# 22 fp32 products of constants per layer, placed at five points between the gating unit and the recurrence

## The chip, the cores and the metric

The kernel runs on one core of one Trainium2 chip. The metric is the device time of one launch in microseconds (us), as the median of several runs. TensorE multiplies matrices into PSUM (8 banks of 128 x 512 fp32), VectorE and ScalarE do the elementwise work and copy out of PSUM, SyncE and GpSimd issue DMAs. The engines run their own instruction streams in order and wait for one another on semaphores.

## The reference

A two-layer block (attention, mLSTM, windowed attention) is followed by a second two-layer block, the last block here. Only the middle of each of its layers matters. From the projection `h = x @ w_in` three units are formed side by side:

```
out_a = spatial_gating(gelu(a_u), gelu(a_v), ...)      # layer_norm over 256 features, then w (4 heads, 128x128) @ v
out_b = gated_deltanet(...)                            # (I + L)^-1 by a triangular solve, then a recurrence over chunks
out_c = gla(...)                                       # gated linear attention: chunk states, masked scores, outputs
mix   = concatenate([out_a, out_b, out_c]) @ w_out
```

Everything is fp32 with 512 tokens and a width of 1024. The kernel solves the delta rule with chunks of 128 tokens, 8 heads: 32 triangular matrices of 128 x 128 for each layer.

## The kernel before

The program is a list of stages. Each stage has one function for TensorE, one for ScalarE, one for VectorE; after most of them stands a barrier (`end_stage`: drain, count, wait for all three). The GEMMs of the projections and of the MLPs (`gemm_pe`, L513 and L515) split fp32 into two parts and are the bulk of the time. The order of work in the stages around the change is written out by hand.

In the last block each layer `l` runs: projection, `form_pe` (L2340, the decayed key products and the matrices L), then one stage with `units_pe` and `solve_pe` on TensorE, `compact`, `units_act` and `solve_act` on ScalarE and `solve_dve` on VectorE, and then `rec_pe` (the recurrence, L2565 to L2601, with L2569 its first products).

`units_pe` (L2144) does in this order:

- L2147: two products with a matrix of ones give the sums over features of the gating unit; VectorE centres with them (L2221, L2223), ScalarE squares (L2202).
- L2151: two products of ones give the sums of squares; ScalarE makes the reciprocal root (L2205, L2206), VectorE normalises (`norm_v_dve`, L2236, L2237).
- L2156, L2161: transposes of the normed values and of the decayed keys, copied by ScalarE (L2213 to L2216).
- L2167: the seven state updates of the gated attention, read by VectorE (`gla_states_dve`, L2265, L2270).
- L2171, L2176: the gating unit's bias rows (2 rows deep) and its mixing products.
- L2183: the scores of the gated attention, 32 rows deep, masked by VectorE (`gla_mask_dve`, L2282), after a wait for the states.
- L2190, L2194: its outputs.

`solve_pe` (L2380) waits for the inverses of the 32 x 32 diagonal blocks (`so_x`), which VectorE computes row by row (`rows_dve_of_inverse`, L2509 and L2511) in between all the above and transposes at L2532. It then puts the inverse of 128 x 128 together: 32 x 32 products (L2385, L2386, L2395 to L2397), then 64 x 64 products (L2412 forms one off-diagonal part, L2403 in `corner` the next), with copies by ScalarE and VectorE (L2454, L2461, L2467, L2542, L2547) in between.

`keep_busy_pe` (L530) is already there: after the row sums that close a GEMM it runs six fp32 products of the constant matrix of ones with 512 columns of constants (L533) into a PSUM bank that nobody reads.

Of the kernel before, what the change touches and what calls it, by code (L numbers as in the profile page):

```python
# [231 lines left out]
def program(nc, xT_d, vec_d, shared_d, first_d, second_d, gup_d, sguw_d, sgub_d, crow_d, ada_d, w_d, out_d):  # L232
    with ExitStack() as ctx:
# [3 lines left out]
        def signal(name):  # L237
            return Signal(ctx.enter_context(nc.semaphore(name)))
# [26 lines left out]
        def C(name, i=0, n=P):  # L265
            if name in SHARED_AT:
                return con[:, SHARED_AT[name] + i:SHARED_AT[name] + i + n]
            at = FIRST_AT[name] if name in FIRST_AT else SECOND_AT[name]
            return con2[:, at + i:at + i + n]

        def area(at, *dims, of=arena):

            n = int(np.prod(dims))
            assert at + n <= ARENA, (at, n)
            a = of[:, at:at + n]
            if len(dims) == 2:
                return a.rearrange("p (a b) -> p a b", a=dims[0])
            if len(dims) == 3:
                return a.rearrange("p (a b c) -> p a b c", a=dims[0], b=dims[1])
            return a  # L280
# [246 lines left out]
                if "unread" in tiles[-1]:  # L527
                    keep_busy_pe(pe, tiles[-1]["unread"])

        def keep_busy_pe(pe, bank):  # L530

            for _ in range(6):
                pe.matmul(PS[:, bank, :], C("ones"), con[:, 0:512], start=True, stop=True)  # L533

        def together(tiles, n):
# [1587 lines left out]
        def vt(n, cols):  # L2123

            return Y[:, 6 + n // 2, 256 * (n % 2) + cols.start:256 * (n % 2) + cols.stop]

        bc = ada_extra[:]
        _, e1, e2, kdec = (area(4096 + 512 * i, 512) for i in range(4))
# [11 lines left out]
        def update_bank(c):  # L2140

            return PS[:, UPDATE_BANKS[c % 2][c // 4], 256 * (c // 2 % 2):256 * (c // 2 % 2) + 256]

        def units_pe(pe, l):  # L2144

            for t in range(2):
                ins = pe.matmul(PS[:, 0, :], C("ones"), vp_[:, t, :], start=(t == 0), stop=(t == 1))  # L2147
            ins.then_inc(sg_z.sem, 1)
            pe.wait_ge(sg_sq.sem, sg_sq.next("pe"))
            for t in range(2):  # L2150
                ins = pe.matmul(PS[:, 1, :], C("ones"), sq2[:, t, :], start=(t == 0), stop=(t == 1))  # L2151
            ins.then_inc(sg_t.sem, 1)
            pe.wait_ge(sg_v.sem, sg_v.next("pe"))
            for n in range(NLT):
                for t in range(2):
                    ins = pe.transpose(PS[:, 2 + n // 2, 256 * (n % 2) + P * t:256 * (n % 2) + P * t + P],  # L2156
                                       vp_[:, t, P * n:P * n + P], C("ident"))
            ins.then_inc(sg_t.sem, 1)
            pe.wait_ge(ga_prod.sem, ga_prod.next("pe"))
            for n in range(NLT):  # L2160
                ins = pe.transpose(PS[:, 5, P * n:P * n + P], kdec[:, P * n:P * n + P], C("ident"))  # L2161
            ins.then_inc(ga_kt.sem, 1)
            pe.wait_ge(sg_tc.sem, sg_tc.next("pe"))
            pe.wait_ge(ga_ktc.sem, ga_ktc.next("pe"))
            for c in range(7):
                o, n = 64 * (c % 2), c // 2
                ins = pe.matmul(update_bank(c), kdt[o:o + 64, n, :], vg[o:o + 64, n, :], start=True, stop=True)  # L2167
            ins.then_inc(ga_st.sem, 1)
            pe.wait_ge(sg_w.sem, sg_w.next("pe"))
            for q in range(2):  # L2170
                pe.matmul(PS[:, q, :].rearrange("p (n t) -> p n t", n=NLT), PAIR[0:2], bs_row[0:2, P * q:P * q + P].unsqueeze(1).to_broadcast([2, NLT, P]),  # L2171
                          start=True, stop=False, skip_group_check=True)
                for n in range(NLT):
                    for j in range(2):
                        h = 2 * q + j
                        ins = pe.matmul(PS[64 * j:64 * j + 64, q, P * n:P * n + P], vt(n, slice(64 * h, 64 * h + 64)), wsT[:, h, :],  # L2176
                                        start=False, stop=True, skip_group_check=True)
            ins.then_inc(sg_z.sem, 1)
            pe.wait_ge(ga_state.sem, ga_state.next("pe"))
            for h in range(4):  # L2180
                for n in range(NLT):
                    a, b = 32 * h, P * n
                    ins = pe.matmul(PS[:, GS[h], b:b + P], kg[a:a + 32, b:b + P], qg[a:a + 32, b:b + P], start=True, stop=True)  # L2183
                ins.then_inc(ga_s.sem, 1)
            pe.wait_ge(ga_pt.sem, ga_pt.next("pe", 4))
            for n in range(NLT):
                for p in range(2):
                    for j in range(2):
                        h = 2 * p + j
                        ins = pe.matmul(PS[64 * j:64 * j + 64, 6 + p, P * n:P * n + P], vg[:, n, 64 * h:64 * h + 64],  # L2190
                                        pTg[:, n, P * h:P * h + P], start=True, stop=False, skip_group_check=True)
                    for c in (2 * n, 2 * n + 1):
                        if c >= 1:
                            ins = pe.matmul(PS[:, 6 + p, 64 * c:64 * c + 64], Sg[:, c, P * p:P * p + P], qg[:, 64 * c:64 * c + 64],  # L2194
                                            start=False, stop=True, skip_group_check=True)
            ins.then_inc(ga_o.sem, 1)
# [116 lines left out]
        def lt(h, n, rows, cols):  # L2313

            return XH[rows, 2 * h + n // 2, P * (n % 2) + cols.start:P * (n % 2) + cols.stop]
# [8 lines left out]
        def quad(q):  # L2324
            return slice(32 * q, 32 * q + 32)
# [52 lines left out]
            so_L.advance("pe", 8)  # L2378

        def solve_pe(pe):  # L2380
            pe.wait_ge(so_x.sem, so_x.next("pe"))
            for g in range(2):
                for m in range(16):
                    h, n, i = 4 * g + m // 4, m % 4, 16 * g + m
                    pe.matmul(PS[quad(1), g, 32 * m:32 * m + 32], lt(h, n, quad(0), quad(1)), X64[quad(0), i, 0:32], start=True, stop=True)  # L2385
                    ins = pe.matmul(PS[quad(3), 2 + g, 32 * m:32 * m + 32], lt(h, n, quad(2), quad(3)), X64[quad(2), i, 0:32],  # L2386
                                    start=True, stop=True)
                ins.then_inc(so_y.sem, 1)
            pe.wait_ge(so_T.sem, so_T.next("pe"))
            pe.wait_ge(ga_out.sem, ga_out.next("pe"))  # L2390
            for g in range(2):
                pe.wait_ge(so_yc.sem, so_yc.next("pe", 2))
                for m in range(16):
                    i = 16 * g + m
                    pe.matmul(PS[quad(1), 4 + g, 32 * m:32 * m + 32], T32[quad(1), i, :], Y32[quad(1), i, :], start=True, stop=True)  # L2395
                    pe.matmul(PS[quad(2), 6 + g, 32 * m:32 * m + 32], Y32[quad(3), i, :], T32[quad(3), i, :], start=True, stop=True)
                    ins = pe.matmul(PS[quad(0), 4 + g, 32 * m:32 * m + 32], Y32[quad(1), i, :], T32[quad(1), i, :], start=True, stop=True)  # L2397
                ins.then_inc(so_off.sem, 1)

            def corner(r):  # L2400
                pe.wait_ge(so_zc.sem, so_zc.next("pe"))
                for m in range(8):
                    ins = pe.matmul(PS[LOW, 4 + r, 64 * m:64 * m + 64], Y64[TOP, 8 * (r % 2) + m, :], lt(2 * r + m // 4, m % 4, TOP, TOP),  # L2403
                                    start=True, stop=True)
                ins.then_inc(so_top.sem, 1)

            for r in range(4):
                if r % 2 == 0:
                    pe.wait_ge(so_offa.sem, so_offa.next("pe"))
                    pe.wait_ge(so_offv.sem, so_offv.next("pe", 2))  # L2410
                for m in range(8):
                    ins = pe.matmul(PS[TOP, r, 64 * m:64 * m + 64], lt(2 * r + m // 4, m % 4, LOW, TOP), X64[LOW, 8 * r + m, :],  # L2412
                                    start=True, stop=True)
                ins.then_inc(so_z.sem, 1)
                if r >= 1:
                    corner(r - 1)
            corner(3)

        so_d, so_ld, so_T = (signal(n) for n in ("solve_blocks_compact", "solve_blocks_in", "solve_inverses32_turned"))
        D_ = area(4096, 4, 512)[:, :, 0:256]  # L2420
# [488 lines left out]
```

## Time and profile before

| | |
|---|---|
| median of 3 timed runs | 3948.94 us (3947.5 to 3950.69) |
| the profiled execution | 3947.25 us, span 3945.5 us |
| TensorE busy | 3780.2 us, 96% |
| VectorE / ScalarE busy | 2107.3 / 1392.4 us |
| mean granted TensorE clock | 0.961 |
| L513, three largest groups | 2080.0 + 1755.8 + 1206.1 us |
| L533 (products of constants) | 72 records, 31.9 us |

One execution is profiled; times count from its start. Busy time of an engine is time with an instruction under way; idle time of an engine that isn't waited for costs nothing. A matmul record of fp32 covers half of a product: one `matmul` call shows as two records. The granted clock is given as a share of 2.4 GHz; it has two levels here, 1.00 (2.4 GHz) and 0.50 (1.2 GHz), and a mean over a stretch may lie between.

### The profile page before, as it was taken

How to read it: one execution, taken by the hardware profiler on the slowest of the kernel's cores; microseconds unless marked ns; L12 is line 12 of the kernel's file. 1: busy time of each engine (PE TensorE's matmuls, PEld its weight loads, DVE VectorE, ACT ScalarE, POOL GpSimd, SP SyncE). 2: the span in 40 equal slices, each digit the busy share in tenths (PEclk: the TensorE clock that was granted, in tenths of full speed). 3: DMA queues.
4: the chain of work that ended last, by engine and by line, in shares of the span. 5: the costliest groups of instructions: out<-in, count | busy, mean ns of one | idle time of the engine just before them, and what ended most of it. 6: DMA issues, size and time to landing. Idle time of an engine off the chain costs nothing.

```text
span 3945.5 us, 45029 instructions
## 1 busy us (share of the span) xinstructions
PE 3780.2 (96%) x18676; PEld 3145.5 (80%) x18676; DVE 2107.3 (53%) x3730; ACT 1392.4 (35%) x2109; POOL 86.1 (2%) x164
## 2 busy tenths in 40 slices
PE   8997989999999999999999979999999999899998
PEld 5985669999987688888887867888788877677886
DVE  5936767644457543333337477533633374765335
ACT  4424552212356432322226533222322256233222
POOL 0100001111000000000000000000000000000000
PEclk9998999999999999999999959999999999689999
DMA  6410004333220122232222201222222222002222
GB/s 221 153 50 1 22 27 134 123 127 129 102 69 23 43 96 96 96 110 98 99 96 83 80 6 43 96 97 96 88 96 96 98 84 80 22 33 89 98 97 80
DMA packets 92887, 333.37 MB, mean 84 GB/s; under 512 B 11364, under 2 KB 11532, under 8 KB 92428
## 3 DMA queue, kind: packets, MB, share of 16 engines
q1 hardware_dynamic: 77040, 278.10, 20.5%
q0 software_dynamic: 12800, 41.95, 3.4%
q10 hardware_dynamic: 2844, 10.44, 0.7%
q8 instruction: 148, 2.42, 0.2%
q14 instruction: 55, 0.45, 0.0%
HBM read 328.35 MB, written 2.10 MB: 84 GB/s over the span
## 4 chain that ended last, share of the span: by engine, by line
PE 88%; DVE 5%; ACT 5%; issue 1%; DMA 0%; DVEq 0%; ACTq 0%; SPq 0%
PE PS L513 73%; PE PS L1111 2%; PE PS L515 2%; PE PS L1129 1%; PE PS L1656 1%; PE PS L1468 1%; PE PS L1096 1%; PE PS L1099 0%; PE PS L956 0%; PE PS L1097 0%; PE PS L2565 0%; PE PS L2357 0%; PE PS L1439 0%; PE PS L726 0%; PE PS L2194 0%
## 5 line engine op out<-in xcount | busy, mean ns | idle before, releaser
L513 PE MATMUL PS<-arena_r,ring_hi 128*128 128x512 f32 (+1 forms) x6160 | 2080.0, 376 | 45.8 <-DVE H_r L690 38.9
L513 PE MATMUL PS<-arena_r,ring_r 128*128 128x512 f32 (+1 forms) x4688 | 1755.8, 375 | 0.0
L513 PEld LDWEIGHTS PS<-arena_r,ring_hi 128*128 128x128 f32 x6160 | 1153.4, 188 | 227.9 <-DVE H_r L690 30.0
L513 PE MATMUL PS<-H_r,ring_hi 128*128 128x512 f32 (+1 forms) x3216 | 1206.1, 375 | 0.0
L513 PEld LDWEIGHTS PS<-arena_r,ring_r 128*128 128x128 f32 x4688 | 883.4, 188 | 130.7
L382 DVE TENSOR_TENSOR ring_r<-ring,ring_hi 128x1024 fp32r<-128x1024 f32 x514 | 627.1, 1222 | 652.5 <-ACT ring_hi L373 652.0
L373 ACT ACTIVATE ring_hi<-ring 128x1024 fp32r<-128x1024 f32 x514 | 541.4, 1055 | 866.9 <-DMA ring<-weights_dram 859.0
L513 PEld LDWEIGHTS PS<-H_r,ring_hi 128*128 128x128 f32 x3216 | 608.3, 189 | 94.8 <-issue 3.1
L1825 ACT ACTIVATE arena<-PS 128x512 f32<-128x512 f32 x88 | 52.6, 598 | 527.5 <-PE PS L513 527.5
L1275 DVE SCALAR_TENSOR_TENSOR XH<-PS,mods,XH 128x256 f32<-128x256 f32 (+1 forms) x168 | 79.4, 518 | 235.9 <-PE PS L513 221.3
L344 DVE CAST arena_r<-arena 128x512 fp32r<-128x512 f32 (+1 forms) x184 | 74.2, 404 | 199.0 <-ACT arena L1322 195.9
L1829 DVE SCALAR_TENSOR_TENSOR arena<-arena,PS 128x512 f32<-128x512 f32 x88 | 60.5, 687 | 219.6 <-PE PS L513 219.6
L1321 ACT ACTIVATE arena<-PS 128x384 f32<-128x384 f32 (+1 forms) x96 | 49.9, 520 | 282.0 <-PE PS L513 282.0
L1836 DVE SCALAR_TENSOR_TENSOR XH<-XH,PS 128x512 f32<-128x512 f32 x64 | 44.0, 687 | 153.9 <-PE PS L513 153.9
L1293 DVE TENSOR_TENSOR arena_r<-arena,arena_r 128x512 fp32r<-128x512 f32 (+1 forms) x184 | 118.9, 646 | 6.3
L1111 PE MATMUL PS<-arena 128*128 128x512 f32 (+1 forms) x184 | 92.4, 607 | 4.7 <-ACT arena L1197 4.7
L690 DVE TENSOR_TENSOR H_r<-XH,arena_r 128x512 fp32r<-128x512 f32 (+1 forms) x144 | 91.1, 633 | 4.9
L1129 PEld LDWEIGHTS PS<-con,arena 128*128 128x128 f32 x368 | 43.1, 143 | 49.6 <-issue 39.1
L1146 DVE TENSOR_REDUCE small<-PS 128x1 f32<-128x768 f32 (+3 forms) x80 | 61.6, 770 | 30.3 <-PE PS L1099 28.8
L1184 ACT ACTIVATE arena<-PS,small 128x768 f32<-128x768 f32 (+3 forms) x80 | 59.4, 743 | 38.2 <-DVE small L1151 38.0
L1859 DVE SCALAR_TENSOR_TENSOR arena<-arena,vec 128x511 f32<-128x511 f32 (+2 forms) x72 | 53.5, 748 | 36.0 <-ACT arena L1874 34.3
L344 DVE CAST arena_r<-XH 128x512 fp32r<-128x512 f32 (+1 forms) x144 | 56.4, 391 | 20.1 <-ACTq L326 17.7
(389 smaller groups left out, 3347.1 us busy)
## 6 DMA issues: line engine op xcount, KB each, us to landing
ring<-weights_dram SPq DMA_DIRECT2D x526, 512.0 KB, 3.2
rstd<-ada_later_dram POOLq DMA_DIRECT2D x54, 256.0 KB, 2.9
mean<-ada_later_dram POOLq DMA_DIRECT2D x53, 256.0 KB, 3.0
ada_extra<-ada_later_dram POOLq DMA_DIRECT2D x53, 256.0 KB, 3.0
XH<-xT_dram ACTq DMA_DIRECT2D x1, 3072.0 KB, 20.4
ring<-weights_dram ACTq DMA_DIRECT2D x4, 512.0 KB, 4.1
out_dram<-XH SPq DMA_DIRECT2D x8, 256.0 KB, 2.0
con<-second_dram ACTq DMA_DIRECT2D x1, 1536.0 KB
```

Source lines behind the costliest of these rows:

```text
L344: return nc.vector.tensor_copy(out, src)
L373: nc.scalar.activation(ring_hi[:, n % RING, :, :], ring[:, n % RING, :, :], ACT.Copy).then_inc(hi_ready.sem, 1)
L382: nc.vector.tensor_tensor(ring_lo[:, slot, :, :], ring[:, slot, :, :], ring_hi[:, slot, :, :].bitcast(F32), ALU.subtract).then_inc(lo_read ...
L513: ins = pe.matmul(PS[:, o.bank, 0:hi - lo], w[:, 0, :], x, **flags)
L515: ins = pe.matmul(PS[:, o.bank, 0:t["n"] * P], x, w.rearrange("p a b -> p (a b)"), **flags)
L690: nc.vector.tensor_tensor(H_r[:, k, lo:hi], x, x_hi.bitcast(F32), ALU.subtract).then_inc(xlo_ready.sem, 1)
L1111: ins = pe.matmul(out_of(gi), g["v"](kts[t]), turned[gi % 2][:, t, :], start=(t == 0), stop=(t == len(kts) - 1))
L1129: ins = pe.transpose(turned_ps, p_tile, C("ident"))
L1146: v_link(dve, nc.vector.tensor_reduce(col(i, 0), s_all(i, g), AX, ALU.max))
L1275: ins = nc.vector.scalar_tensor_tensor(out=X[:, m, a:b], in0=ps[:, a - lo:b - lo], scalar=mods[:, l, s, gate + m:gate + m + 1], in1=X[:, m ...
L1293: nc.vector.tensor_tensor(h_lo(lo, hi), h(lo, hi), h_hi(lo, hi).bitcast(F32), ALU.subtract).then_inc(hidden_ready.sem, 1)
L1829: return nc.vector.scalar_tensor_tensor(out=h[:, m, :], in0=h[:, m, :], scalar=0.5, in1=ps, op0=ALU.mult, op1=ALU.mult)
```

## The change

`keep_busy_pe` gets a count `n`, six by default, and is called at five more places in each of the two layers: 3, 6 and 7 products into bank 4 in `units_pe`, 4 into bank 5 at the head of `solve_pe`, 2 into bank 0 at its end, 22 in all. Each call stands just ahead of a wait, the last one ahead of the barrier. Nothing reads what they write, and no wait and no signal is added.

```diff
-        def keep_busy_pe(pe, bank):
+        def keep_busy_pe(pe, bank, n=6):
-            for _ in range(6):
+            for _ in range(n):
                 pe.matmul(PS[:, bank, :], C("ones"), con[:, 0:512], start=True, stop=True)
...
                 ins = pe.matmul(PS[:, 0, :], C("ones"), vp_[:, t, :], start=(t == 0), stop=(t == 1))
             ins.then_inc(sg_z.sem, 1)
+            keep_busy_pe(pe, 4, 3)
             pe.wait_ge(sg_sq.sem, sg_sq.next("pe"))
             for t in range(2):
                 ins = pe.matmul(PS[:, 1, :], C("ones"), sq2[:, t, :], start=(t == 0), stop=(t == 1))
             ins.then_inc(sg_t.sem, 1)
+            keep_busy_pe(pe, 4, 6)
             pe.wait_ge(sg_v.sem, sg_v.next("pe"))
...
             ins.then_inc(sg_z.sem, 1)
+            keep_busy_pe(pe, 4, 7)
             pe.wait_ge(ga_state.sem, ga_state.next("pe"))
...
         def solve_pe(pe):
+            keep_busy_pe(pe, 5, 4)
             pe.wait_ge(so_x.sem, so_x.next("pe"))
...
             corner(3)
+            keep_busy_pe(pe, 0, 2)
```

## Rows read from the trace of the kernel before

**Rows 1.** The page: granted clock in 40 equal slices, and the chain by engine.
```profile
PEclk9998999999999999999999959999999999689999
PE 88%; DVE 5%; ACT 5%; issue 1%; DMA 0%; DVEq 0%; ACTq 0%; SPq 0%
```

**Rows 2.** Windows, layer 0: stretch, its length, busy us (records) by engine, clock, DMA.
```profile
2294.00:2299.00 5.00, 3.78 (x4) 1.17 (x4) 3.63 (x5) 1.66 (x4) 0.00 (x0) 0.50 0.01 3
2299.00:2302.00 3.00, 0.00 (x0) 0.00 (x0) 2.83 (x8) 1.06 (x2) 0.00 (x0) 0.97 0.00 0
2302.00:2306.00 4.00, 3.37 (x4) 0.97 (x4) 3.39 (x11) 1.82 (x3) 0.00 (x0) 0.57 0.00 0
2306.00:2309.40 3.40, 0.00 (x0) 0.00 (x0) 1.05 (x2) 3.37 (x7) 0.00 (x0) 1.00 0.00 0
...
2332.80:2345.40 12.60, 12.54 (x61) 8.96 (x61) 11.71 (x29) 1.06 (x1) 0.00 (x0) 0.50 0.01 1
2345.40:2353.00 7.60, 7.19 (x321) 6.98 (x320) 5.74 (x9) 5.04 (x8) 0.00 (x0) 0.50 0.02 5
2353.00:2365.20 12.20, 12.08 (x128) 11.89 (x128) 3.06 (x6) 2.87 (x6) 0.00 (x0) 0.50 0.00 1
...
2381.00:2384.50 3.50, 3.50 (x32) 3.34 (x31) 1.43 (x4) 0.77 (x2) 0.00 (x0) 0.99 0.00 0
```

**Rows 3.** Windows, layer 1, the same columns.
```profile
3401.70:3405.00 3.30, 0.23 (x1) 0.23 (x2) 3.13 (x8) 1.42 (x3) 0.00 (x0) 1.00 0.00 0
3405.00:3408.40 3.40, 3.27 (x4) 0.74 (x3) 3.02 (x11) 1.11 (x2) 0.00 (x0) 0.51 0.00 0
...
3435.00:3448.20 13.20, 12.58 (x62) 9.00 (x64) 12.31 (x29) 1.06 (x1) 0.00 (x0) 0.50 0.01 1
```

**Rows 4.** Timeline, TensorE: start, length, instruction, shapes, records; at full clock.
```profile
1370.95 5.31 PE L533 MATMUL PS<-con 128*128 128x512 f32 x12
```

**Rows 5.** Timeline, TensorE, layer 0; in brackets idle time before it.
```profile
2294.99 3.78 PE L2147 MATMUL PS<-arena,con 128*128 128x512 f32 x4 [1.43 <-DVEq L326]
2302.14 3.37 PE L2151 MATMUL PS<-XH,con 128*128 128x512 f32 x4 [3.37 <-ACT XH L2202]
2310.82 1.97 PE L2156 MATMUL PS<-con,arena 128*128 128x128 f32 x8 [5.31 <-DVE arena L2237]
...
2314.54 3.75 PE L2167 MATMUL PS<-arena 64*128 64x256 f32 x14 [0.90 <-ACT arena L2216]
2318.22 2.07 PE L2171 MATMUL PS<-scratch,con_r 2*128 2x512 f32 x2
...
2326.03 5.13 PE L2183 MATMUL PS<-arena 32*128 32x128 f32 x32
2332.86 0.70 PE L2190 MATMUL PS<-arena 128*64 128x128 f32 x4 [1.70 <-DVE arena L2282]
```

**Rows 6.** Timeline, VectorE, layer 0.
```profile
2318.40 2.22 DVE L2265 TENSOR_TENSOR arena<-PS,con 128x512 f32<-128x512 f32 x4 [1.74 <-PE PS L2167]
...
2330.33 2.48 DVE L2282 TENSOR_TENSOR arena<-PS,con 128x512 f32<-128x512 f32 x4
...
2342.10 1.95 DVE L2532 STREAM_TRANSPOSE arena<-silu_ctx 128x1024 f32<-128x1024 f32 x1
```

**Rows 7.** Chain in order of time, end of the solve and recurrence: start, length, what.
```profile
2362.10 3.06 PE PS L2403 x29
...
2365.97 1.86 PE PS L2569 x8
2367.84 3.60 PE PS L2565 x16
...
2377.57 1.97 PE PS L2601 x16
...
2382.28 1.73 PE PS L2565 x16
...
2385.20 1.02 PE PS L2601 x16
```

## The prediction

> **What bounds the kernel now.** I read the page first: TensorE is busy nearly all the span, 88% of the chain of waits is TensorE, and the granted clock is 1.00 (2.4 GHz) nearly everywhere except in two dips of the slices, one for each layer of the last block [rows 1]. So a TensorE product added anywhere is paid for, unless it lands in a wait of TensorE, and the only thing that products with unread results can give back is the granted clock of their neighbours. The change puts all 22 products of a layer inside those dips. Then I read layer 0 in stretches (layer 1 repeats it 1102.6 us later, with the same dips): while the gating unit's two ones products ran, and after them, the clock went from 0.50 to 0.97 with TensorE standing still, fell again during the next two products, and stayed at 0.50 (1.2 GHz) all the way to the recurrence [rows 2, 3]. Third, the timeline of TensorE with what ended each wait [rows 5], and last the VectorE instructions that release it [rows 6], because VectorE's inversion of 32x32 blocks (small instructions back to back) runs beside all of this and is what TensorE waits for.
>
> Times below are those of layer 0 in the profiled execution. It took 3947.25 us around a span of 3945.5; the median of the three timed runs is 3948.94, so it stands 1.7 us below.
>
> **Price of one product.** It is fp32, so it shows as two records. At 2.4 GHz 12 records took 5.31 us, the last one alone 0.59: (5.31 - 0.59) / 11 = 0.43 us a record, 0.86 us a product [rows 4]. At 1.2 GHz the same shape (L2147, L2151) took 3.78 and 3.37 us for two products with the tail [rows 5]; I take 1.71, twice the fast price. 22 products are 18.9 us a layer at full clock and 37.6 at half, against waits of TensorE of 3.37, 5.31, 0.90 and 1.70 us in this stretch [rows 5]. So they do not fit the waits as they stand: the change lives on the clock it buys. It adds no semaphore wait and nothing reads banks 4, 5 and 0 in between; but TensorE works in order, so whatever stands behind a product waits for it, and with it ScalarE and VectorE.
>
> **Part 1, 3 products before the wait for the squares.** L2147 ends at 2298.77, L2151 starts at 2302.14: 3.37 us of cover [rows 5]. The clock is up from about 2299.2 (0.97 over 2299 to 2302) [rows 2]; 3 x 0.86 = 2.6, and some 0.3 more for the first one at half clock: over at 2301.7, hidden. All at half clock they would take 5.1 and push 1.8 into the chain. With TensorE busy instead of still I expect the clock to hold through L2151, whose 3.37 us shrink to 1.9. ScalarE's root and VectorE's normalisation follow directly: -1.5 us.
>
> **Part 2, 6 products before the wait for the normed values.** L2151 now ends at 2304.0, the wait ends 1.5 earlier than before, at 2309.3; 6 x 0.86 = 5.2 ends at 2309.2. Hidden with nothing to spare; at half clock it would be late by 5. Behind it the transposes (L2156, L2161) and the state updates (L2167, 3.75 us) run at full clock, about 1.0 and 1.7 us shorter. What then is late is VectorE: before L2265 it sat idle for 1.74 us [rows 6]. That wait goes too, so L2265 starts 1.5 + 1.7 = 3.2 us earlier, at 2315.2. More can't be had there, since VectorE is then without a break up to its transposes of the inverse.
>
> **Part 3, 7 products before the wait for the states.** In the trace of before there is no wait at this place: L2183 starts where L2176 ends [rows 5]. There will be one only if the stretch L2171 to L2176 (7.8 us, 2318.22 to 2326.03) shrinks with the clock. At full clock I take 4.2: over at 2318.3, products 6.0 more, 2324.3, then L2183 in 2.8 instead of 5.13: 2327.1. VectorE reaches the first L2282, at 2330.33 before, at 2327.1 [rows 6]. Just hidden; gain still 3.2 us, no more, because VectorE sets it.
>
> **Part 4, 4 products before the wait for the inverse.** This is the step that decides. From 2327.1 to 2329.7 TensorE again stands still, after 32-row products. Before, in both layers, the clock fell in or just after the 3 us in which TensorE stood still at full clock [rows 2, 3], so I let it fall here, at about 2330. L2190 and L2194 then start at 2329.7 and run their 12.5 us at half clock, as in both layers before: TensorE busy for 12.54 of 12.60 us, clock 0.50 throughout, and no rise [rows 2, 3]. They end at 2342.2 and not at 2345.4. VectorE has the inverse ready (L2532 ended at 2344.05) at 2340.9 [rows 6]: TensorE is late already, there is no wait, and the 4 products stand wholly in the chain. 3.4 us at full clock, 6.8 at half; full-size products did raise the clock each time after 3 to 4 us [rows 2], so I take 5.5 us: L2385 starts at 2347.7, +2.3 us against before.
>
> The Trainium skill, page "TensorE: Matmul & The Clock Gate", part 1, section "What's actually happening", says that "the default state is throttled, and activity releases the throttle". Read as busy time that is against the row of L2190: busy without a break, and never released. Read so, the four products and all after them would run at full clock, and the sum would be rival B or A below.
>
> **Part 5, the solve.** Its first half is 32x32 products, 321 records in 7.19 us busy, 22 ns apart [rows 2]; between them stand ScalarE's copies. Bounds: nothing to 1.9 us if the clock is still full (half of a start part of 3.8 us); I take 0.5, since no row shows these records at full clock. The second half, 64x64 products, 12.08 of 12.20 us busy at 0.50 before [rows 2], keeps its length: such products never raised the clock, and after 32x32 products I expect it to fall. Bounds: 0 to 5 us of gain; I take 0.
>
> By the same page, section "Wait — 56ns, not 53.3ns?", the start-to-start of matmuls never drops under about 25 ns however small they are; by that the first half would gain exactly nothing. The trace has them at 22, so the rule does not hold here to the nanosecond, and by it the sum would be 0.5 us a layer larger.
>
> **Part 6, 2 products at the end.** Cover is what VectorE's last L2547 and the barrier take: from the end of L2403 at 2365.16 to L2569 at 2365.97, 0.8 us [rows 7]. The barrier waits for TensorE to drain, so all three engines wait. At half clock 3.4 + 0.1 - 0.8 = +2.7, at full clock +1.0. Return: if the clock rises after them, L2565 takes 1.73 and not 3.60 us, as it does later in the recurrence [rows 7], and L2569 loses up to 0.9. It comes part of the time and only for part of the stretch, because L2569 is eight tiny products: I take -1.5. Net +1.2.
>
> **Sum.** A layer: +2.3 - 0.5 + 1.2 = +3.0 us; two layers +6.0; 3947.25 + 6.0 = 3953.3. The moments at which the clock changes need not lie alike in other executions; that is worth a microsecond or three either way, more than the 1.7 us between the profiled run and the median, so I leave it at 3953.
>
> **Rivals.**
>
> A, full clock from L2147 to the recurrence: L2190/L2194 in 6.4 us, over at 2336.1, 4 products until 2339.5, L2385 with the inverse at 2340.9 (-4.5); the 64x64 products 5 us shorter; end products +1.0; L2569 and L2565 -2.8; L2601 1.02 for 1.97 [rows 7] and L2582 behind it by nearly as much, -1.7. That is -13 a layer, 3921. For it: the counts of products fill exactly the waits that this timeline has. Against: 12 us each of L2190 and of L2403 busy at 0.50. The page's rule named above is this rival.
>
> B, the clock holds through L2190 and is lost in the solve: -4.5 + 1.2 = -3.3 a layer, 3941. For it: the recurrence held 0.99 with products of the same kind, L2565 and L2601 [rows 2, 7]. Against: the 2.6 us of standing still just ahead.
>
> D, on the slower side: the clock is lost in part 2's tail, during the 1.3 us in which TensorE waits for ScalarE's copies ahead of L2167. Then L2265 starts at 2315.9, L2171 to L2176 need their 7.8 us until 2323.5, and the 7 products start at half clock: 3 us until the rise and 4.5 after, 2331.0, then L2183 2.8: 2333.8, the masks end at 2334.4 (2332.81 before). L2190 starts 1.6 late; some 2 us of it at full clock give 2 back, then the 4 products: L2385 at 2350.3, +4.9, and with parts 5 and 6 +5.6 a layer, 3958. It decides from the point where L2183 ends after VectorE has reached L2282. For it: before, the clock fell in just such a stretch, a wait with work beginning after it (0.57 over 2302 to 2306) [rows 2]. The extreme, no rise at all in any place, is 37.6 us a layer less what waits cover, over 20 a layer; against that stands the rise at 2299.
>
> **How the numbers follow.** Forecast 0.45 (3947 to 3957), A 0.07, B 0.18, D 0.25, something worse 0.05. A measurement of this kernel tells about 0.2%, 7.9 us, from no change, that is below 3941.0 or above 3956.8. Faster: A and half of B and a little, 0.20. Slower: most of D, the worse case and the forecast's upper edge, 0.32. Same: 0.48. The range that leaves out A, the worst and the edge of D is 3938 to 3965.
>
> **What would show it.** Right: clock near 1.00 from 2299 to about 2329, L2151 near 1.9 us, L2265 about 3 us earlier, 0.50 over L2190, and no idle time after the 4 products ahead of L2385, which starts 2 us late; L2569 2 to 5 us late. Wrong, towards faster: L2190/L2194 under 10 us, or a wait of TensorE before L2385. Wrong, towards slower: 0.50 over L2171 and an L2183 that VectorE waits for.

## The result, and the profile after

The change takes 3953.62 us, median of 20 runs, against 3947.55 us before, 20 runs on the same chips: ratio 1.0018, 95% interval [1.0012, 1.0024], 6.1 us slower. The forecast was 3953. Single runs of either kernel fall in two groups some 8 us apart (before: 3938 to 3942 and about 3948; after: 3945 to 3946 and 3952 to 3957), and two of the profiles below, e3's and e7's, show the difference ahead of layer 0, in code that all these kernels share, so where a few microseconds matter I read the profiles by layer as well. The profiled execution took 3953.63 us, its span is 3951.8.

L2147 keeps its number, those behind it are shifted: L2151 is L2152, L2156 is L2158, L2167 is L2169, L2171 is L2173, L2176 is L2178, L2183 is L2186, L2190 and L2194 are L2193 and L2197, L2385 is L2389, L2403 is L2407, L2412 is L2416, L2569 is L2574, L2565 is L2570, L2601 is L2606; on VectorE L2265 is L2268, L2282 is L2285, L2532 is L2537.

The timeline of TensorE in layer 0 after, which answers to [rows 5]:

```profile
2298.44 3.03 PE L533 MATMUL PS<-con 128*128 128x512 f32 x6
2302.01 1.98 PE L2152 MATMUL PS<-XH,con 128*128 128x512 f32 x4 [0.55 <-ACT XH L2205]
2303.84 5.31 PE L533 MATMUL PS<-con 128*128 128x512 f32 x12
2309.31 1.09 PE L2158 MATMUL PS<-con,arena 128*128 128x128 f32 x8 [0.16 <-DVE arena L2240]
...
2312.16 1.96 PE L2169 MATMUL PS<-arena 64*128 64x256 f32 x14 [1.32 <-ACT arena L2219]
...
2318.20 6.28 PE L533 MATMUL PS<-con 128*128 128x512 f32 x14
2324.41 2.82 PE L2186 MATMUL PS<-arena 32*128 32x128 f32 x32
2329.64 0.65 PE L2193 MATMUL PS<-arena 128*64 128x128 f32 x4 [2.42 <-DVE arena L2285]
...
2341.99 6.04 PE L533 MATMUL PS<-con 128*128 128x512 f32 x8
2347.96 0.21 PE L2389 MATMUL PS<-arena,XH 32*32 32x32 f32 x1
...
2367.70 3.45 PE L533 MATMUL PS<-con 128*128 128x512 f32 x4
2371.23 1.05 PE L2574 MATMUL PS<-arena,con_r 8*128 8x4 f32 x8
```

Three things are to be seen. The first three groups of products (3.03, 5.31, 6.28 us) have gone into waits: behind the first two TensorE still waits 0.55 and 0.16 us, behind the third not at all, because L2186 follows at once. Where no product was put it waits 1.32 us (ahead of L2169) and 2.42 us (ahead of L2193). The fourth group (6.04 us) has no wait behind it: L2389 follows at once. And the last stands between the solve and the recurrence, 3.45 us where the barrier had left 0.8 us [rows 7].

VectorE, which answers to [rows 6], has no idle time before L2268 any more, and everything on it is 3.2 us earlier:

```profile
2315.17 2.22 DVE L2268 TENSOR_TENSOR arena<-PS,con 128x512 f32<-128x512 f32 x4
...
2327.11 2.48 DVE L2285 TENSOR_TENSOR arena<-PS,con 128x512 f32<-128x512 f32 x4
...
2338.89 1.95 DVE L2537 STREAM_TRANSPOSE arena<-silu_ctx 128x1024 f32<-128x1024 f32 x1
```

The windows after, which answer to [rows 2], with the same columns (the clock is the third number from the right):

```profile
2302.00:2326.00 24.00, 22.51 (x112) 12.28 (x113) 21.42 (x51) 7.11 (x11) 0.00 (x0) 1.00 0.00 1
2326.00:2329.70 3.70, 1.28 (x18) 1.09 (x17) 3.70 (x7) 0.00 (x0) 0.00 (x0) 1.00 0.00 0
2329.70:2342.00 12.30, 12.30 (x61) 8.84 (x61) 11.41 (x28) 1.06 (x1) 0.00 (x0) 0.50 0.00 0
2342.00:2348.00 6.00, 6.00 (x11) 2.35 (x13) 4.19 (x6) 0.00 (x0) 0.00 (x0) 0.60 0.00 0
2348.00:2353.20 5.20, 4.50 (x318) 4.24 (x317) 0.85 (x2) 3.82 (x6) 0.00 (x0) 1.00 0.03 8
2353.20:2355.50 2.30, 0.10 (x7) 0.06 (x3) 0.52 (x1) 1.24 (x2) 0.00 (x0) 0.59 0.00 0
2355.50:2367.80 12.30, 12.30 (x132) 12.12 (x132) 3.42 (x5) 2.96 (x5) 0.00 (x0) 0.50 0.00 1
2367.80:2371.20 3.40, 3.35 (x4) 1.07 (x4) 0.68 (x1) 0.00 (x0) 0.00 (x0) 0.58 0.00 0
2371.20:2374.10 2.90, 2.87 (x24) 2.82 (x24) 0.00 (x0) 0.57 (x2) 0.00 (x0) 1.00 0.03 6
2374.10:2380.00 5.90, 4.11 (x13) 2.93 (x12) 4.94 (x9) 0.39 (x1) 0.00 (x0) 0.50 0.00 1
2380.00:2384.00 4.00, 3.67 (x24) 3.34 (x25) 1.03 (x3) 0.00 (x0) 0.00 (x0) 0.50 0.00 0
```

The clock is full over all of the first two windows, falls at the very start of L2193, comes back late in the four products, holds over the 32x32 products, is low over the 64x64 ones, and is up again for just the 2.9 us of L2574 and L2570.

To compare runs I count from the start of L2147 in each layer (all starts read from the timelines; the last column is the copy of the recurrence's outputs, L2655 before):

| layer 0 / layer 1 | L2190 starts | L2385 starts | L2412 starts | L2569 starts | L2655 starts |
|---|---|---|---|---|---|
| before | 37.9 / 38.0 | 50.4 / 50.5 | 58.1 / 58.4 | 71.0 / 71.3 | 102.6 / 102.7 |
| after | 34.8 / 34.8 | 53.1 / 53.1 | 60.8 / 61.2 | 76.4 / 76.6 | 105.7 / 105.9 |

Gained 3.1 us up to L2190, lost 5.8 from there to L2385 (net 2.7), nothing changed up to L2412, lost 2.7 more at the barrier (5.4), and got 2.3 back in the recurrence: 3.1 and 3.2 us a layer, 6.3 in all, which is the 6.3 us between the two spans.

### The profile page after: what moved, and what is told of

Its sections match the earlier page's. It is cut to its first block, busy times and chain, and to the rows that moved or that the text cites. A ratio compares the mean times of both kernels' runs of the same rounds, so it can differ in the third digit from the quotient of the medians.

```text
span 3951.8 us, 45205 instructions
## 1 busy us (share of the span) xinstructions
PE 3797.4 (96%) x18764; PEld 3143.1 (80%) x18764; DVE 2107.6 (53%) x3730; ACT 1393.4 (35%) x2109; POOL 86.4 (2%) x164
## 4 chain that ended last, share of the span: by engine, by line
PE 88%; DVE 6%; ACT 4%; issue 1%; PEld 1%; DMA 0%; PEldq 0%; DVEq 0%; ACTq 0%; SPq 0%
PE PS L513 73%; PE PS L1111 2%; PE PS L515 2%; PE PS L1129 1%; PE PS L1656 1%; PE PS L1468 1%; PE PS L1096 1%; PE PS L956 0%; PE PS L1099 0%; PE PS L1097 0%; PE PS L2360 0%; PE PS L726 0%; PE PS L1439 0%; PE PS L2197 0%; DVE H_r L690 0%
## 5 line engine op out<-in xcount | busy, mean ns | idle before, releaser
L533 PE MATMUL PS<-con 128*128 128x512 f32 x160 | 80.1, 652 | 0.0
```

## The experiments

All are the changed kernel with other counts; "3, 6, 7, 4, 2" names the five calls in order. Each was timed in five rounds beside the kernel before, whose median in the three sets (e1 to e4, e5 to e8, e9 to e11) was 3946.5, 3946.6 and 3946.4 us. "Measured" below is the difference from that median. The last column adds up, over both layers, how much later or earlier than before L2655 starts: it leaves out whatever differs outside of the two layers.

| run | calls | median us | ratio to before, 95% | L2385 starts | L2655 starts | two layers, us |
|---|---|---|---|---|---|---|
| e1_36 | 3, 6 | 3939.88 | 0.9982 [0.9974, 0.9991] | 47.3 / 47.3 | 99.3 / 99.2 | -6.7 |
| e2_367 | 3, 6, 7 | 3943.04 | 0.9990 [0.9980, 0.9999] | 47.3 / 47.2 | 101.3 / 101.2 | -2.8 |
| e3_3674 | 3, 6, 7, 4 | 3950.51 | 1.0008 [0.9999, 1.0018] | 51.5 / 53.1 | 105.7 / 105.9 | +6.3 |
| e4_3672 | 3, 6, 7, -, 2 | 3946.33 | 0.9999 [0.9991, 1.0008] | 47.2 / 47.3 | 102.6 / 101.6 | -1.1 |
| e5_only4 | 4 alone | 3959.72 | 1.0027 [1.0016, 1.0038] | 56.4 / 56.4 | 108.4 / 108.4 | +11.5 |
| e6_only2 | 2 alone | 3949.27 | 1.0006 [0.9995, 1.0017] | 50.4 / 50.6 | 102.1 / 105.8 | +2.6 |
| e7_fill | 3, 6, 7, +3, 4, 2 | 3936.50 | 0.9973 [0.9964, 0.9981] | 47.2 / 46.0 | 100.0 / 98.9 | -6.4 |
| e8_fill_no42 | 3, 6, 7, +3 | 3939.68 | 0.9985 [0.9976, 0.9993] | 46.0 / 46.0 | 99.1 / 98.7 | -7.5 |
| e9_fill_no2 | 3, 6, 7, +3, 4 | 3938.87 | 0.9982 [0.9973, 0.9992] | 46.0 / 46.0 | 98.7 / 98.6 | -8.0 |
| e10_fill1 | 3, 6, 7, +1, 4, 2 | 3953.31 | 1.0020 [1.0008, 1.0031] | 53.1 / 53.1 | 105.7 / 105.8 | +6.2 |
| e11_fill_rec | 3, 6, 7, +3, 4, and 2 in the recurrence | 3937.48 | 0.9986 [0.9976, 0.9995] | 46.0 / 46.0 | 97.6 / 98.0 | -9.6 |

### Which of the five calls gains and which loses

**e1_36**, the gating unit's two calls alone:

```diff
-            keep_busy_pe(pe, 4, 7)
-            keep_busy_pe(pe, 5, 4)
-            keep_busy_pe(pe, 0, 2)
```

> Only the 3 and the 6 products of the gating unit; no 7, 4 and 2. Theory (parts 1 and 2 gain about 3.2 us a layer and all that follows gives it away): L2265 starts 3.2 us earlier than before, L2190 and L2385 3.2 us earlier, total -6 us (0.9985). Rival 1 (the 7 products, which stand where no wait was, are needed to hold the clock, or are the loss): then without them L2183 runs late and the total is 0 to -2 us. Rival 2 (the full clock in the gating unit is given back by a VectorE that is busy throughout): total 0.

Measured -6.6 us. The 3 and the 6 gain all that there is to gain with these five calls. TensorE (same columns as above) now waits before the scores and before the outputs:

```profile
2316.25 1.09 PE L2178 MATMUL PS<-con,XH 128*64 128x128 f32 x16
2319.64 5.13 PE L2185 MATMUL PS<-arena 32*128 32x128 f32 x32 [2.29 <-DVE arena L2272]
...
2328.70 0.69 PE L2192 MATMUL PS<-arena 128*64 128x128 f32 x4 [3.93 <-DVE arena L2284]
```

The scores are back at 5.13 us, half clock, and it does not matter: VectorE is not ready for them earlier. Both rivals fall.

**e2_367**, the same with the line of the 7 kept:

> The 3, 6 and 7 products; no 4 and 2. Theory: the 7 are hidden wholly behind VectorE; L2190 starts 3.2 us earlier than before as without them, L2385 2342.2, total -6 us, same as with 3 and 6 alone within 1 us. Rival 1 (the 7 are the loss): total 0 to +6 us.

Measured -3.5, not -6. Up to L2385 the two are alike (47.3 and 47.3). They part in the recurrence: its products begin 0.7 us later, because the solve took 0.6 us longer with no wait that the profile names, and the clock rises 3.4 us later. The clock's rise is read from windows over the first products of the recurrence, e1_36 and then e2_367, both from 79 us after the start of L2147 on:

```profile
2373.00:2376.50 3.50, 3.10 (x21) 2.77 (x22) 0.68 (x2) 0.00 (x0) 0.00 (x0) 0.50 0.00 0
2376.50:2380.00 3.50, 3.50 (x33) 3.50 (x31) 1.54 (x4) 0.65 (x2) 0.00 (x0) 0.99 0.00 0
```

```profile
2373.00:2376.40 3.40, 2.50 (x19) 2.18 (x20) 1.17 (x3) 0.00 (x0) 0.00 (x0) 0.50 0.00 0
2376.40:2379.80 3.40, 3.40 (x18) 3.40 (x17) 0.84 (x2) 0.00 (x0) 0.00 (x0) 0.50 0.00 0
2379.80:2383.00 3.20, 3.20 (x31) 2.92 (x32) 1.79 (x5) 0.77 (x2) 0.00 (x0) 1.00 0.00 0
```

In the second stretch one kernel got 33 matmul records through and the other 18. So the 7 products are hidden where they stand, and the 2 us a layer that these profiles differ by lie 50 us later, in when the clock rises. That is not yet a price of the 7: e8 below has them too, starts the recurrence at 67.4 / 66.8 us and ends at 99.1 / 98.7, as e1 does. The late rise goes with the late start of the recurrence, and why e2's solve took longer stays open. The intervals of the two ratios overlap as well, and -3.5 us lies between the theory (-6) and rival 1 (0 to +6).

**e3_3674 and e4_3672**, the change without the 2 and without the 4:

```diff
-            keep_busy_pe(pe, 0, 2)      # e3_3674
-            keep_busy_pe(pe, 5, 4)      # e4_3672
```

> The change without the 2 products at the end of the solve. Theory: L2385 starts 2.6 us later than before, the recurrence's first products 2.6 us later, nothing given back by L2570: total +5 us (1.0013). Rival 3 (the 2 products ahead of the barrier are the loss): total -2 to 0.

> The change without the 4 products ahead of the inverse. Theory: L2385 starts at 2342.2 and not at 2348.0, 5.8 us a layer earlier than with the change; the 2 products add 2.7 us at half clock and L2574/L2570 may give back up to 2.5: total -3 to -6 us against before. Rival 3 (the 2 are the loss): total 0 to +3. Rival 1: as the change, +6.

Measured +4.0 and -0.2 us, where the change is at +6.1 against its own set: taking the 4 away takes off 6.2 us, taking the 2 away 2.0. By layer it is 7.4 and nothing. e3 came about as expected, though the interval of its time reaches down to -0.4 and so nearly to rival 3. e4 came less well, -0.2 and not -3 to -6, because the 2 gave back only part and e2, its base, was itself at -3.5; its interval (-3.6 to +3.2) holds rival 3 as well as the upper part of the theory. In layer 1 of e3's profile the recurrence starts 2.3 us earlier than with the 2 (74.3 against 76.6), yet ends at the same 105.9. Its layer 0 has L2385 at 51.5, because the clock fell 1.1 us into L2190 and not at its start.

**e5_only4 and e6_only2**, each of them alone on the kernel before:

> Only the 4 products ahead of the inverse. Theory: TensorE is bound there, so they stand wholly in the chain, at half clock at first: L2385 starts 5 to 6 us later (50.4 after L2147 before, 55.5 to 57 now), little comes back: total +8 to +12 us (1.0020 to 1.0030). Rival (their clock pays for them in the solve): 0 to +3 us.

> Only the 2 products ahead of the barrier. Theory: L2569 2.6 us later in each layer; what comes back hangs on whether the clock rises before L2565 and how early it rises again in the recurrence, where before it rose 3.5 us after L2601 began: total 0 to +5 us, +3 likeliest. Rival (the clock of L2565 pays for them): -2 to 0.

Measured +13.1 us, a little above the +8 to +12 expected (+11.5 in the two layers), and +2.6 us, near the +3 expected; the interval, -2 to +7, does not shut out its rival (-2 to 0), which the two layers (+2.6) speak against. For e5 the timeline and window of TensorE at the four products:

```profile
2345.14 6.21 PE L533 MATMUL PS<-con 128*128 128x512 f32 x8
2351.29 0.21 PE L2386 MATMUL PS<-arena,XH 32*32 32x32 f32 x1
```

```profile
2344.30:2351.30 7.00, 7.00 (x14) 3.18 (x14) 4.99 (x6) 0.70 (x1) 0.00 (x0) 0.57 0.00 0
```

Six microseconds at a clock of 0.57 over the window, none of it hidden: L2385 went from 50.4 to 56.4. That is the price of full-size products that lift the clock where TensorE itself is the bound. e6 shows how much hangs on luck: layer 0 ended 0.5 us earlier than before (the clock rose with the 2), layer 1 3.1 us later (it did not).

### Why the clock was lost before L2190

The theory was that TensorE's standing still ahead of L2190 loses the clock, and that products like L2190's, which never raised it, can hold it. **e7_fill** puts 3 more products into that wait, into bank 6, which is free until L2190 writes it:

```diff
...
+            keep_busy_pe(pe, 6, 3)
             pe.wait_ge(ga_pt.sem, ga_pt.next("pe", 4))
```

> The change with 3 more products, into bank 6, in the 2.4 us in which TensorE waits for the masked scores after L2186. Theory (the clock fell only since TensorE stood still there; small products after it can hold it for a while): L2190 begins at full clock and ends 3 to 5 us earlier, the 4 products then need 3.4 us and lie in the wait for the inverse: L2385 starts 46 to 48 after L2147 (53.1 with the change, 50.4 before), total -2 to -8 us against before. Rival (products like L2190 lose the clock whatever stands before): L2190 as with the change, total +6 us or more, since 2.6 us do not fit 2.4.

Measured -10.1 us, the lowest median of all, and beyond the -2 to -8 expected. The median says too much. The profiled execution is 15.9 us shorter than that of before, but 9.6 us of these are there before the first L2147 starts (2285.4 against 2295.0), in code that both share. The two layers give 2.6 and 3.8 us, 6.4 together, where the change loses 6.3. So the three more products turn the change's loss into a gain, but into one no larger than that of the 3 and the 6 alone (6.7 us). The timeline of its layer 1, TensorE, and the windows over the same stretch:

```profile
3414.91 2.82 PE L2186 MATMUL PS<-arena 32*128 32x128 f32 x32
3417.65 2.84 PE L533 MATMUL PS<-con 128*128 128x512 f32 x6
3420.43 0.44 PE L2194 MATMUL PS<-arena 128*64 128x128 f32 x4
...
3427.55 3.65 PE L533 MATMUL PS<-con 128*128 128x512 f32 x8
3431.41 0.21 PE L2390 MATMUL PS<-arena,XH 32*32 32x32 f32 x1 [0.21 <-DVE arena L2538]
```

```profile
3417.60:3420.40 2.80, 2.80 (x8) 1.06 (x6) 2.80 (x6) 0.00 (x0) 0.00 (x0) 1.00 0.00 0
3420.40:3427.20 6.80, 6.80 (x58) 4.94 (x58) 6.20 (x17) 0.00 (x0) 0.00 (x0) 1.00 0.00 0
3427.20:3431.40 4.20, 4.00 (x12) 1.73 (x12) 3.91 (x10) 0.01 (x1) 0.00 (x0) 1.00 0.01 2
3431.40:3433.70 2.30, 2.21 (x128) 2.10 (x128) 2.27 (x2) 2.00 (x3) 0.00 (x0) 1.00 0.03 7
```

L2190 and L2194, 12.5 us at half clock in the change, now take 7.3 at full clock. The same 4 products, 6.04 us and late in the change, are 3.65 us here and end before VectorE has the inverse: TensorE waits 0.21 us for it. So the same line of code is a loss or free by the clock that it meets. The three products themselves start L2190 0.3 us late (35.1 for 34.8). Layer 0 came less well: the clock had fallen once more during L2178, the 7 products took 7.05 us, L2190 started at 36.5 and L2385 at 47.2; from there on L2190, L2194 and the 4 products ran at full clock too. The rival falls.

**e8_fill_no42**, the same without the 4 and the 2:

> 3, 6, 7 and the 3 more into bank 6, without the 4 and the 2. Theory: L2190 partly at full clock, so that TensorE is done before the inverse and VectorE sets L2385: 45.9 after L2147 (47.2 with 3, 6 and 7 alone), 1.3 us better than those a layer: total -7 to -10 us. Rival: L2190 all at half clock, total as with 3, 6 and 7 alone, -3 us.

Measured -7.0 us, L2385 at 46.0 in both layers as expected: VectorE sets it now. The rival falls, because L2190 and L2194 took 7.3 us in both layers.

**e10_fill1**, 1 product in place of 3:

> The change with 1 more product into bank 6 and not 3. Theory (what decides is how long TensorE stands still before L2190): with 0.86 us of the 2.4 us filled the clock falls near the start of L2190 as with the change in most runs, total +3 to +7 us against before. Rival (any full-size product there will do): as with 3, -10 us.

Measured +6.9 us, and L2190 at half clock again, with L2385 back at 53.1, as expected; the rival, that any full-size product there will do, falls:

```profile
2326.37 1.13 PE L533 MATMUL PS<-con 128*128 128x512 f32 x2
...
2341.23 6.02 PE L533 MATMUL PS<-con 128*128 128x512 f32 x8
```

```profile
2328.90:2340.40 11.50, 11.50 (x57) 8.04 (x57) 10.61 (x28) 0.32 (x1) 0.00 (x0) 0.50 0.00 0
```

Two products more or less, 1.7 us of TensorE time in a wait, decide over 12.6 us in the two layers (the medians say 16.8, with e7's early start in them). All eight layers with the 3 more (e7, e8, e9, e11) ran L2190 and L2194 at full clock; in all ten with one or none behind the 7 (after, e2, e3, e4, e10) the clock fell within 1.2 us of the start of L2190. So what TensorE does in this wait causes the loss in part 4. Whether standing still or the want of full-size products does it is not separated: the wait was only ever filled with full-size ones.

**e9_fill_no2** (e7 without the 2) and **e11_fill_rec** (e9 with 2 products in the recurrence, in its first chunk before the wait `re_qd`):

> The change with the 3 more products into bank 6, without the 2 ahead of the barrier. Theory (the 2 cost 2.6 us at half clock and get about as much back from the first products of the recurrence): L2569 2.6 us earlier than with them, the end of the recurrence within 1 us, total within 2 us of the run with them (3936.5). Rival (the 2 are a loss of 2.6 us a layer): total 5 us lower, 3931. Rival (they are a gain): 2 to 5 us higher.

> As the first of these three, with 2 products into bank 0 in the recurrence's first chunk, in the 2.1 us that TensorE waits for VectorE's decayed keys. Theory: the clock rises up to 3.4 us earlier in the recurrence, where products at half clock take 1.8 times as long: 1 to 1.5 us gained a layer against 0 to 1.3 us by which 2 products at half clock outlast the wait: total -2 to +1 us against the first of these three. Rival (the rise does not come earlier): +2.6 us.

Measured -7.5 and -8.9 us. The median of e9 is 2.4 us above e7's, which by itself would be the second rival, but e7's median is too low for the reason given above, and the medians of e7, e9 and e11 cannot be told apart by their intervals. By layer the profiles say: without the 2 the recurrence starts 2.9 us earlier and ends 0.3 us earlier than with them (98.6 for 98.9 in layer 1), a draw as expected (in layer 0 e7 was 1.2 us late already at L2385); with the 2 in the recurrence the clock rises before L2601, whose first eight records take 0.66 us there and 1.12 in e9, and the layer ends 1.1 and 0.6 us earlier than e9's; the last line of each fence below is L2601's first eight records, e11_fill_rec and then e9_fill_no2:

```profile
2370.31 3.61 PE L533 MATMUL PS<-con 128*128 128x512 f32 x4
2373.85 0.66 PE L2607 MATMUL PS<-arena 128*64 128x128 f32 x8
```

```profile
2371.55 1.12 PE L2606 MATMUL PS<-arena 128*64 128x128 f32 x8 [2.12 <-DVE arena L2645]
```

## Why the prediction was right, step by step

**Price of a product.** 0.86 us at full clock: six took 5.31 us, seven 6.28. Right.

**Part 1.** L2152 took 1.98 us (1.9 forecast), with 0.55 us of the wait left. **Part 2.** L2268 started at 2315.17 (2315.2). e1 shows the two as the only gain: -6.6 us. **Part 3.** The 7 ended at about 2324.5 (2324.3), L2186 took 2.82 (2.8), the masks started at 2327.11 (2327.1). Hidden, as said. Why e2, which has them, ends its layers 2 us later than e1 is open; e8, which has them too, does not.

**Part 4.** The clock fell at about 2329.7, L2193 and L2197 ran at 0.50, the 4 products took 6.04 us and not 5.5, and L2385 came 2.7 us later than before where 2.3 was forecast. The fall had been let happen from two rows of TensorE standing still; e7 and e10 show that what TensorE does in that wait was the cause, and e7 shows rival B's first step, the clock held through L2190, as a kernel. I had written against B "the 2.6 us of standing still just ahead": that wait is what decided.

The Trainium skill, page "TensorE: Matmul & The Clock Gate", section "Why this matters for your kernels", advises to leave no long idle gaps between bursts of matmuls. The trace agrees that the gap matters, but the gap here, 2.42 us, is shorter than those that the section warns of: the clock was lost behind it for all of L2193 and L2197, and kept where the gap was filled. As for the sentence "activity releases the throttle" of the Trainium skill, same page, section "What's actually happening", it stands as before: L2193 and L2197, busy for 12.30 of 12.30 us at 0.50, released nothing.

**Part 5.** Forecast 0.5 us of gain from the 32x32 products; none came, L2412 is 2.7 us late as L2385 is. This is the place where the forecast missed a term: it had nothing that stops TensorE inside the solve. The products did gain: the first half of the solve up to the last of them ran at 1.00. But then TensorE stood still with no semaphore to wait for. The chain in order of time, layer 0 and layer 1 (start, length, what):

```profile
2353.13 2.31 issue
...
3458.93 2.28 issue
```

It stands just ahead of the last of L2400 and L2401. Before, the same stretch had 0.67 us in layer 1 and nothing in layer 0. In e5, also at full clock but with 32 records fewer ahead of it in each layer, no standstill is longer than 0.8 us, and from L2385 to L2412 it took 6.5 us and not 7.7: that is the gain that the change did not get. The floor of about 25 ns from start to start that the Trainium skill gives (page "TensorE: Matmul & The Clock Gate", section "Wait — 56ns, not 53.3ns?"), which I had weighed here, does not hold for these products, which go by turns to two 32x32 corners of the array (`quad(1)` and `quad(3)` in `solve_pe`): the window of e7 from 3431.4 on has 128 records in 2.21 us busy, 17 ns apart, against 27 for the same 128 before, at half clock. The 64x64 products kept their length, 9.0 us from the first to the last L2412 in both kernels, as forecast.

**Part 6.** +2.7 forecast at half clock, 2.6 measured (L2569 from +2.7 to +5.4). The return was 2.3 us and not 1.5: L2574 1.05 for 1.86, L2570 about 1.9 for 3.60, but the clock was low again at 2374.1 and rose 3.4 us later in the recurrence than before (89.5 for 86.1). Net +0.4 in this profile, where 1.2 was forecast. The runs do not agree on its size: by medians 1.0 (e3 against the change), 1.6 (e4 against e2) and 1.3 (e6) a layer, by layers 0, 0.9 and 1.3.

**Sum.** +3.0 a layer forecast, 3.1 and 3.2 measured. Three small errors nearly cancelled: part 4 came 0.4 dearer and part 5 gave 0.5 less, part 6 cost 0.8 less. So the path is right, and that the total is met within 0.1 us is luck. The range of 3938 to 3965 holds 3953.62. The part "same" of the forecast was 0.48; 6.1 us is within the 7.9 that I had called no change, though 20 runs tell it from zero.

## What to carry to other kernels

Dummy products pay only in a wait of TensorE that is as long as they are at the clock they meet: count their price at both clocks, and look for what TensorE does just ahead. A chain of fillers is only as good as its one gap left open: here 1.7 us more of filler in a 2.4 us wait turned 6.2 us of loss in the two layers into 6.4 of gain. What they can give ends where another engine sets the pace: nine products a layer (e1) got 6.7 us, 25 (e7) 6.4. Where TensorE has no wait, as ahead of the inverse at half clock, do not put any: alone they cost 13.1 us.

## What the runs showed that was not expected

- Products that never raise the clock can hold it: L2190 and L2194 ran 12.5 us at 0.50 in the change, where the clock was lost ahead of them, and 7.3 us at 1.00 in all eight layers in which three full-size products stood directly ahead of them.
- The 2.3 us of "issue" at full clock among 32x32 records. The trace shows a 16 KB load of the instruction queue from 2352.81 to 2353.95, and others before and after it, so TensorE may have run out of instructions. In e7, e9, e10 and e11 a standstill of 1.9 to 2.2 us likewise begins 0.4 to 0.5 us after such a load starts, in both layers. But before has such a load at 2351.86 too, in the same half of the solve at half clock, and no standstill over 0.5 us in that layer. The cause is inferred, no run tested it.
- The moment at which the clock rises in the recurrence was 82.6, 86.1 and 89.5 us after the start of L2147 in e1, e2 and after; from e1 to e2 a layer ends 2 us later with it.
